# Attention scores over all 128 rows with zero-filled key tiles, and half blocks in both expert tables

## The reference

```python
# MLA branch, 8 heads, query and key 128 + 64 wide
q = concat([q[..., :128], rope(q[..., 128:])]); k = concat([kv[..., :128], k_rope])
# differential branch, 8 heads, two maps of width 64 per head
p = causal_probs(q1, k1) - lam * causal_probs(q2, k2)
# experts: the 16 best of 128 x 128 for each of 8 heads and token
a = gelu(einsum('chkd,cd->chk', expert_u[ec], hc)); w = gates * a
out = einsum('chk,chkd->cd', w, expert_v[ec])
# third layer: 32 query heads, 4 key heads of width 64, window of 128, with sinks
```

## Time and profile before

| | before |
|---|---|
| median of three runs | 3079.28 us (3079.03 to 3079.35) |
| profiled execution | 3080.09 us, its span 3078.3 us |
| PE busy | 3047.7 us (99%) |
| PE weight loads busy | 2492.5 us (81%) |
| DVE busy | 2023.4 us (66%) |
| ACT busy | 1501.2 us (49%) |
| GpSimd busy | 554.1 us (18%) |
| DMA | 587.99 MB, 191 GB/s on the mean |

### The profile page before, as it was taken

The page is one execution under the profiler, slowest core; times in us unless marked ns, Lnnn a source line. Parts: engine busy times, 40 slices in busy tenths (PEclk is TensorE's granted clock), DMA queues, the critical chain, the costliest instruction groups (busy, mean ns, idle before and its releaser), DMA issues.

```text
span 3078.3 us, 44643 instructions
## 1 busy us (share of the span) xinstructions
PE 3047.7 (99%) x14774; PEld 2492.5 (81%) x14774; DVE 2023.4 (66%) x3616; ACT 1501.2 (49%) x2444; POOL 554.1 (18%) x335
## 2 busy tenths in 40 slices
PE   8999999999999999999999999999999999999999
PEld 7888787788888888888877777777778888887787
DVE  4567677656877777655555555555565776678865
ACT  4445464554545454544444444444464445556554
POOL 0000000000088878787000000000000000000000
PEclk9999999999999999999999999999999999999999
DMA  7777554566577777777676666666666556654355
GB/s 236 256 255 240 165 164 144 165 186 206 171 180 183 182 183 183 182 187 193 206 233 208 212 210 208 211 208 226 188 188 195 179 163 190 192 180 135 107 159 179
DMA packets 198300, 587.99 MB, mean 191 GB/s; under 512 B 54688, under 2 KB 55328, under 8 KB 197136
## 3 DMA queue, kind: packets, MB, share of 16 engines
q1 hardware_dynamic: 149920, 539.82, 56.1%
q0 software_dynamic: 47936, 46.06, 7.4%
q10 hardware_dynamic: 304, 0.30, 0.0%
HBM read 565.00 MB, written 21.10 MB: 190 GB/s over the span
## 4 chain that ended last, share of the span: by engine, by line
PE 57%; DVE 1%; DMA 0%; ACT 0%; issue 0%; SPq 0%; DVEq 0%; ACTq 0%
PE bank L602 8%; PE bank L604 8%; PE bank L603 8%; PE bank L903 8%; PE bank L902 8%; PE bank L901 8%; PE bank L831 6%; PE bank L832 3%; PE bank L667 1%; PE bank L572 1%; PE bank L679 0%; DMA raw<-in_w_v 0%; DVE lo L1503 0%; PE bank L690 0%; PE bank L689 0%; PE bank L688 0%
## 5 line engine op out<-in xcount | busy, mean ns | idle before, releaser
L1503 DVE TENSOR_TENSOR lo<-raw,hi 128x512 fp32r<-128x512 f32 (+2 forms) x1530 | 1313.6, 870 | 911.1 <-ACT hi L1064 899.8
L1064 ACT ACTIVATE hi<-raw 128x512 fp32r<-128x512 f32 (+2 forms) x1530 | 1181.8, 775 | 1470.9 <-PE bank L604 624.0
L831 PE MATMUL bank<-xt,hi 128*128 128x512 f32 x2304 | 818.9, 399 | 5.5 <-DVE lo L1503 4.9
L602 PE MATMUL bank<-hi,xt 128*128 128x512 f32 (+1 forms) x1924 | 766.4, 398 | 6.8 <-DVE lo L1503 6.6
L604 PE MATMUL bank<-hi,xt 128*128 128x512 f32 (+1 forms) x1924 | 750.2, 390 | 0.0
L603 PE MATMUL bank<-lo,xt 128*128 128x512 f32 (+1 forms) x1924 | 748.7, 389 | 0.0
L832 PE MATMUL bank<-xt,lo 128*128 128x256 f32 x2304 | 645.4, 280 | 0.0
L452 POOL DMA_INDIRECT gates_scratch<-picked,place x256 | 497.2, 1942 | 259.0 <-DVE picked L2011 154.6
L831 PEld LDWEIGHTS bank<-xt,hi 128*128 128x128 f32 x2304 | 432.3, 188 | 122.5 <-issue 19.0
L832 PEld LDWEIGHTS bank<-xt,lo 128*128 128x128 f32 x2304 | 435.0, 189 | 0.0
L602 PEld LDWEIGHTS bank<-hi,xt 128*128 128x128 f32 x1924 | 363.0, 189 | 86.6 <-issue 14.5
(11 more groups left out here) (214 smaller groups left out, 1637.7 us busy)
## 6 DMA issues: line engine op xcount, KB each, us to landing
raw<-in_w_u SPq DMA_DIRECT2D x256, 512.0 KB, 3.6
raw<-in_w_v SPq DMA_DIRECT2D x256, 512.0 KB, 3.5
raw<-in_w_ein SPq DMA_DIRECT2D x128, 512.0 KB, 4.1
raw<-in_w_oin SPq DMA_DIRECT2D x72, 512.0 KB, 3.6
raw<-in_w_att SPq DMA_DIRECT2D x64, 512.0 KB, 4.3
raw<-in_w_gate SPq DMA_DIRECT2D x64, 512.0 KB, 3.6
gates_scratch<-u_low POOLq DMA_DIRECT2D x16, 1024.0 KB, 7.5
raw<-in_w_out SPq DMA_DIRECT2D x32, 512.0 KB, 3.7
```

What stands on the lines that cost most here:

```text
L602: pe.matmul(acc, xh, h_[:, s], start=first, stop=False)
L831: pe.matmul(acc[:, :], h_[:, s], xt[:, tile].rearrange("p w t -> p (w t)"), start=first, stop=False)
L1064: act.activation(hi[d][:, c], raw[s][:, c], ACT.Copy).then_inc(hi_ready, 2 // parts)
L1503: dve.tensor_tensor(lo[d][:, c], raw[s][:, c], hi[d][:, c].bitcast(F32), ALU.subtract)\
```

## The change

Four things are done. (1) Scores are always taken over 128 rows. The query tile keeps both of its heads; the key tile exists twice, once with the upper 64 rows zero and once with the lower: `K_LOW` and `K_HIGH`, `KR_LOW` and `KR_HIGH`, `KZ3`. DVE fills them: memsets for the zeros, and for each transposed pair of keys two copies of 64 partitions. (2) In w_u and w_v ACT and DVE split blocks in two halves (the default `parts=2`). (3) `expert_u` and `expert_v` on PE wait for each half and give each half back; in `expert_v` the column half n goes outside and the token half t inside. (4) The scratch of the norm's squares on ACT moves to `NORM_JUNK`, as `K_HIGH` now lies on a part of `JUNK`.

```diff
+        NORM_JUNK = at(90.5, QR)
+        K_LOW, K_HIGH = TT_D[:, 8:16], at(115.5, 8, T)
+        KR_LOW, KR_HIGH = TT[:, 20], at(25, T)
+        KZ3 = at(88, AKV, 2, T)
...
-            return dict(qk=[(TT[:, h], TT[:, 12 + h]), (TT[r, 8 + h // 2], TT[r, 20])],
+            return dict(qk=[(TT[:, h], TT[:, 12 + h]), (TT[:, 8 + h // 2], KR_HIGH if h % 2 else KR_LOW)],
...
-            return dict(qk=[(TT_D[r, h], TT_D[r, 8 + h])],
+            return dict(qk=[(TT_D[:, h], (K_HIGH if w else K_LOW)[:, h])],
...
-            return dict(qk=[(T3[r, h // 2], T3[r, 16 + g])],
+            return dict(qk=[(T3[:, h // 2], KZ3[:, g, h % 2])],
...
                 for q in range(2):
                     b = FIRST["w_u"] + 2 * j + q
-                    pe.wait_ge(lo_ready, 2 * (b + 1) if i is None else i * 8 + 2 * (b + 1))
                     h_, l_ = hi[b % 2], lo[b % 2]
                     for kk in range(8):
+                        if kk % 4 == 0:
+                            there = 2 * b + kk // 4 + 1
+                            pe.wait_ge(lo_ready, there if i is None else i * 8 + there)
...
-                    mm.then_inc(block_used, 2)
+                        if kk % 4 == 3:
+                            mm.then_inc(block_used, 1)
...
-                    for t in range(2):
-                        if first and q == 1 and t == 0:
+                    for n in range(2):
+                        there = 2 * b + n + 1
+                        pe.wait_ge(lo_ready, there if i is None else i * 8 + there)
+                        if first and q == 1 and n == 0:
                             pe.wait_ge(added, N_EXPERT_TILES)
-                        wh, wl = w_hi[j % 2][:, t * P:t * P + P], w_lo[j % 2][:, t * P:t * P + P]
-                        for n in range(2):
+                        for t in range(2):
+                            wh, wl = w_hi[j % 2][:, t * P:t * P + P], w_lo[j % 2][:, t * P:t * P + P]
...
-                    mm.then_inc(block_used, 2)
+                        mm.then_inc(block_used, 1)
...
-                split(b, i, 4, parts=1)
+                split(b, i, 4)
...
+            def turn_halves(low, high, cols):
+
+                n = turns.next()
+                dve.wait_ge(turned, n)
+                dve.tensor_copy(low, bank[4 + n % 2][0:64, 0:cols])
+                dve.tensor_copy(high, bank[4 + n % 2][64:128, 0:cols]).then_inc(turn_out, 1)
...
+                if slot == 13:
+                    dve.memset(K_LOW[64:128].rearrange("p a b -> p (a b)"), 0.0)
+                if slot == 14:
+                    done(dve.memset(K_HIGH[0:64].rearrange("p a b -> p (a b)"), 0.0))
...
+                if slot == 7:
+                    dve.memset(KZ3[64:128, :, 0], 0.0)
+                    done(dve.memset(KZ3[0:64, :, 1], 0.0))
```

More of the change, by code:

```diff
@@ L496, in diff_unit @@
             h, w = u // 2, u % 2
-            r = slice(64 * w, 64 * w + 64)
-            return dict(qk=[(TT_D[r, h], TT_D[r, 8 + h])],
+            return dict(qk=[(TT_D[:, h], (K_HIGH if w else K_LOW)[:, h])],
                         v=[DD[:, t, 2048 + h * 128:2048 + h * 128 + 128] for t in range(2)],
@@ L885, in expert_v @@
                     b = FIRST["w_v"] + 2 * j + q
-                    if i is None:
-                        pe.wait_ge(wlo_ready, j + 1)
-                        pe.wait_ge(lo_ready, 2 * (b + 1))
-                    else:
-                        if q == 0:
-                            pe.wait_ge(wlo_ready, i * 2 + (j + 1))
-                        pe.wait_ge(lo_ready, i * 8 + 2 * (b + 1))
+                    if q == 0:
+                        pe.wait_ge(wlo_ready, j + 1 if i is None else i * 2 + (j + 1))
                     h_, l_ = hi[b % 2], lo[b % 2]
-                    for t in range(2):
-                        if first and q == 1 and t == 0:
+                    for n in range(2):
+                        there = 2 * b + n + 1
+                        pe.wait_ge(lo_ready, there if i is None else i * 8 + there)
+                        if first and q == 1 and n == 0:
                             pe.wait_ge(added, N_EXPERT_TILES)
-                        wh, wl = w_hi[j % 2][:, t * P:t * P + P], w_lo[j % 2][:, t * P:t * P + P]
-                        for n in range(2):
+                        for t in range(2):
+                            wh, wl = w_hi[j % 2][:, t * P:t * P + P], w_lo[j % 2][:, t * P:t * P + P]
                             acc = bank[4 * t + 2 * q + n][:, :]
@@ L1183, in attention @@
                 plain_pair("w_oa", 3)
-            at_junk = JUNK
+            at_junk = NORM_JUNK
             act.dma_start(gain_rows[64:80, :], a["g_norm1"].rearrange("o (k p) -> (o k) p", p=P)).then_inc(gain_in, 16)
@@ L1329, in tile_u @@
                     take_low(j - 1, i)
-                split(b + 1, i, 4, parts=1)
+                split(b + 1, i, 4)
                 if i is None:
@@ L1355, in split_v @@
                 b = FIRST["w_v"] + 2 * j + 1
-                split(b, i, 4 if i is not None else 0, parts=1)
+                split(b, i, 4 if i is not None else 0)
                 if i is not None or j + 1 < N_EXPERT_TILES:
                     high_weights(j + 1, i)
-                split(b + 1, i, 4 if i is not None else 0, parts=1)
+                split(b + 1, i, 4 if i is not None else 0)
             take_low(N_EXPERT_TILES - 1)
@@ L1783, in beside_gate @@
                 if 17 <= slot < 25:
-                    turn_take("diff", TT_D, slot - 17)
+                    j = slot - 17
+                    if j < 4:
+                        turn_take("diff", TT_D, j)
+                    else:
+                        turn_halves(K_LOW[0:64, 2 * j - 8:2 * j - 6].rearrange("p a b -> p (a b)"),
+                                    K_HIGH[64:128, 2 * j - 8:2 * j - 6].rearrange("p a b -> p (a b)"), 2 * T)
                 if slot >= 26:
@@ L1852, in beside_ob @@
                              SIN[:, t], O1[:, 0])
+                    dve.memset(KR_LOW[64:128, :], 0.0)
+                    done(dve.memset(KR_HIGH[0:64, :], 0.0))
                 if slot in (1, 2):
@@ L1859, in beside_ob @@
                 if 5 <= slot < 16:
-                    turn_take("mla", TT, slot - 5)
+                    j = slot - 5
+                    if j < 10:
+                        turn_take("mla", TT, j)
+                    else:
+                        turn_halves(KR_LOW[0:64, :], KR_HIGH[64:128, :], T)
             def take_b(c, i, t, acc):
@@ L2055, in _ @@
             for b in range(2 * ROUTE_TILES):
-                split(FIRST["w_u"] + 1 + b, parts=1)
+                split(FIRST["w_u"] + 1 + b)
                 if b and b % 2 == 0:
@@ L2063, in _ @@
                 for n in range(4):
-                    split(FIRST["w_u"] + 1 + 2 * ROUTE_TILES + n, i, 4, parts=1)
+                    split(FIRST["w_u"] + 1 + 2 * ROUTE_TILES + n, i, 4)
                     if n % 2 == 0:
@@ L2089, in _ @@
                 b = FIRST["w_v"] + 2 * j + 1
-                split(b, parts=1)
+                split(b)
                 if j + 1 < N_EXPERT_TILES:
@@ L2099, in _ @@
                     add_x2(1)
-                split(b + 1, parts=1)
+                split(b + 1)
             def ret_take(h):
@@ L2290, in take_qk @@
                 dve.wait_ge(qk_turned, n)
+                if j >= 8:
+                    g = 2 * (j - 8)
+                    k = bank[7][:, :].rearrange("p (g t) -> p g t", g=2)
+                    dve.tensor_copy(KZ3[0:64, g:g + 2, 0], k[0:64])
+                    dve.tensor_copy(KZ3[64:128, g:g + 2, 1], k[64:128]).then_inc(qk_taken, 1)
+                    return
                 dve.tensor_copy(T3[:, 2 * j:2 * j + 2].rearrange("p a b -> p (a b)"), bank[7][:, :]).then_inc(qk_taken, 1)
```

2 lines of the change are left out of this document (removed).

## The result

The changed kernel takes 3050.72 us, median of 4 runs (3050.61 to 3054.44), against 3079.32 us for the kernel before (3079.03 to 3080.51): a ratio of 0.9911, 95% interval 0.9898 to 0.9923. The gain is 28.6 us where 60 were forecast. The profiled execution took 3050.78 us, its span is 3049.0.

What follows compares the result with a forecast made beforehand. The prediction took TensorE as the bound nearly everywhere. Attention 21, feeding the zero tiles -1, w_v 22 and w_u 18 sum to 60 us; from the profiled 3080.1, 0.8 above the median, that forecasts 3019 us, range 3008 to 3048.

Steps and rivals of the forecast that it cites:

- w_v, 22 us forecast: Table w_v: half blocks bring 256 blocks from 2.81 to 2.72 us, 23 us, less 1 in its first blocks.
- if w_v's matmuls stay 0.234 apart: Sign of being wrong: TensorE's starts in w_v keep their spacing of 0.234 us.
- w_v keeps its pace: Rival: w_v gains nothing from the half blocks, kernel at 3041 us; chance 0.24.
- w_u, 18 forecast: Table w_u: router's part 18.5 us less 2 for router score matmuls, loop 2.5, less 1 for remaining stalls.
- the middle of the two paces of w_qp: w_u's assumed pace with halves: 2.80 us per block, between w_qp's 2.77 and 2.83.
- the upper end given: Upper end of w_u's gain: 26 us, at 2.77 us per block throughout.
- Attention, 21 less 1 forecast: 128-row scores save 10.7 us in sliding windows, 4.8 differential, 5.7 MLA; 1 us goes to feeding the zero tiles.
- The feeding of the zero tiles: DVE's memsets and extra key copies, up to 13 us unhidden: 1 us on the path, 5 at the upper end.
- It still fits: Sliding windows: DVE, 3.2 us busy of a slot shortened to 3.42, 94%, does not hold TensorE back.
- Late scatters: Rival: GpSimd's scatters take 3.2 us each, w_v starts at 1651 not 1500, kernel 3171 us; chance 0.05.
- The halves buy nothing: Rival: in both tables DVE's second instructions come back as lateness, only attention gains, 3059 us; chance 0.06.
- attention gives nothing: Rival: the gaps at attention's scores come from something else than the rows, 3039 us; chance 0.08.

Runs made afterwards that it cites:

- e9: Changed kernel with w_hi and w_lo allocated ahead of hall, on the address grid of hi, lo and xt; 3028.88 us, ratio 0.9829.
- e14: e9 with whole blocks and the old order of the matmuls in w_v; 3039.55 us, ratio 0.9874.
- e3: Changed kernel with whole blocks and the old matmul order in w_v only; five runs, three from 3040.83 to 3041.97 us, two at 3052.45 and 3055.46.
- e2: Changed kernel with whole blocks in both expert tables, so the zero-filled key tiles alone; 3067.82 us, ratio 0.9963.
- e12: Changed kernel with the sliding-window attention as before (keys in 64 rows, no zeros); 3044.41 us.
- e11: Changed kernel without the copy of the sinks in the sliding-window attention after its first three heads, so it computes something else; 3052.73 us.
- e1: Kernel before the change with only the half blocks in both expert tables; 3052.27 us, ratio 0.9918.
- e7: Changed kernel with one odd matmul, of growing size, in every fourth w_u tile from 14 to 82, so it computes something else; 3047.6 us.
- e10: Changed kernel with w_v's stationary tiles shifted stretch by stretch, and w_u's matmuls in pairs or fours with odd matmuls; 3033.44 us.
- e13: e9 with w_u's matmuls in pairs (two of 512 columns, then two of 256) in all tiles; 3019.2 us, ratio 0.9806.

## Why the prediction was right and wrong

**w_v, 22 us forecast, 1.0 measured: the step that failed.** "256 blocks x (2.81 - 2.72) = 23 us" took the evidence that PE's weight loads waited for lo, and that w_gate with halves ran at 2.72, for a cause and its cure. The text named the doubt itself: the starts in w_v are evenly 0.234 apart, not one late and eleven on time. That evenness was the decisive reading, and the forecast's own sign of being wrong ("if w_v's matmuls stay 0.234 apart") is what the trace shows. It was the rival "w_v keeps its pace", given 0.24, that came true, though at 3051 and not at its 3041 us; the other 10 are w_u's and the attentions' shortfall. e9 and e14 show that two things held w_v, each nearly hidden behind the other: the place of the stationary tiles and the late lo. Taking away the second alone gives 1 to 2 us, the first alone 8, both 24. No term of the forecast and none of its rivals had the place of an operand.

**w_u, 18 forecast, 13.7 measured.** The mechanism held: halves took the stalls of the router's part away (2.90 us a block before, 2.827 after) although DVE does 25 us more work there, and the hand-overs cost nothing. The size was off in the pace taken, 2.80, "the middle of the two paces of w_qp". There is no middle: a run has 2.827 or 2.773. At 2.827 the forecast's own sum gives 168 x (2.91 - 2.827) = 14, less its 2 and 1, so 11, and no gain in the loop (measured: none). In a run with the fast pace the gain is 26.5 us (e3: 738.6 down to 712.1), the upper end given (from the first start of w_u's own tiles to the last, 2048 starts in either).

**Attention, 21 less 1 forecast, 13 measured, 11.7 in e2.** The pace of a unit came out as read: scores at 0.65, transposes at 0.33, 1.31 in an MLA unit. The differential units gave 6.0, more than the 4.8: 0.37 us each and not 0.30. Three terms were mis-sized:
- The feeding of the zero tiles, 1 us forecast under the cover of a lo half a block ahead. 2.1 in the sliding windows by e12, and 0.9 more near w_ob by the aligned starts; which instruction there costs it was not tried apart.
- "It still fits", of DVE at 94% in the sliding windows. The 3.75 us per slot divides's 120 us by all 32 units, but only 25 of them start in it, some 4.7 us apart; counted so it is 92%, and 87% were measured. Either sum fits, but the order of DVE's work does not: mask, maxima and lo stand in one queue, and PE's next scores need the maxima. 2.2 us, of which e11 won back 0.9; that all of it is DVE's queue is likely, not shown.
- In MLA the passes gave 5.8 us, as forecast (5.7), and 2.4 were lost again, 2.2 of them where the values wait for ACT's copy. The chain from scores to values has a length of its own, which shorter scores don't shorten.

**The others.** Late scatters: they came 2.13 us apart, as the text worked out against that rival. "The halves buy nothing" and "attention gives nothing" fell with e1 and e2. The range, 3008 to 3048, missed the measured 3050.7, since with w_v at nought (3041) it left only 7 us for all the others together: w_u fell short by 4.3 and attention by 7. Each of the three, w_v 1.0, w_u 13.7 and attention 13 with its feeding, lies within the ends given for it.

## What to carry to other kernels

When an engine's starts are evenly spaced and too far apart, a wait in the same rows is not the cause; removing it pays only once the pace itself is mended. To find what sets a pace, issue one loop in several forms in one run and count instructions per stretch. Before a transformation that saves waits is priced, test where the operands lie: here moving two pairs of tiles in the order of allocation was worth 22 us on top of the half blocks, and 8 without them, where the whole change had brought 28.6.

Where one kernel's runs fall into two groups, compare runs of the same group, or profile both: four runs of the changed kernel showed one of its two times only.

## What the runs showed of the hardware that was not expected

- The distance between the stationary and the moving tile in SBUF sets PE's pace where every matmul has its own weight load, as here: 0.2267 us for 512 fp32r columns at a multiple of 256 bytes, 0.2324 to 0.2343 at 32, 64, 96 and 128, at a granted clock of 1.00. The Trainium skill (SBUF — State Buffer, Operand start alignment) asks only for a start at a multiple of the element size, and says that its runs there timed nothing: legality agrees, time is another matter. The same page (SBUF: two separate sides) has PE never wait on anyone for SBUF. No run here shows PE waiting for another engine's access, but its two own reads are not independent of each other. Why is open.
- Pairs of 512 and 256 columns have two steady paces, 0.3467 and 0.3533 us a pair. A stall or one odd matmul picks one anew, and it holds until the next (18 stretches of e7). Taken as two of 512 and then two of 256 they have one, 0.3483 (e10, e13). The cause is open.
- A change between 128 and 64 rows costs PE twice, at the step itself and again one matmul later. By the starts of the kernel before and of e12 a sliding-window unit loses 0.09 and 0.10 us on the way into the 64-row passes, and 0.09 and 0.06 on the way out to the transposes: 0.34 us. In MLA each change inside the scores costs 0.19.
